# Encoder block on eight cores: the projection's rows transposed by DMA, early weight loads tied to matmuls, another order of the first rows

## What is computed

```python
u = rms_norm(h, g_mix)
z = u @ w_in                                   # value | gate | pool | gate A | gate B, 1024 columns each
gates = sigmoid(z[..., c3:] + b_gate)
a = depthwise_conv31(z_val * sigmoid(z_gate)) + b_dw
y_conv = silu(layer_norm(a)) @ w_conv_out
m = window_mean(z_pool, windows 2, 4, 8, 16 by channel group) - z_pool
y_pool = (per_group(m @ w_pool) * pool_scale) @ w_pool_out
h = h + (gates_A * y_conv + gates_B * y_pool) @ w_o      # output projection
v = rms_norm(h, g_ffn)
h = h + (silu(v @ w_ffn_gate) * (v @ w_ffn_up)) @ w_ffn_down     # hidden width 2816
out = rms_norm(h, g_final)
```

## Time and profile before

| | us |
|---|---|
| kernel, median of 3 runs | 1040.3 (1039.11 to 1068.77) |
| the profiled execution, its own time | 1040.15 |
| its span, slowest core (core 0) | 1038.6 |
| spans of the eight cores | 1034.1 to 1038.6 |
| busy: PE, DVE, ACT, POOL | 1010.3, 429.4, 296.3, 176.6 |

### The profile page before, as it was taken

The page is one execution under the profiler, slowest core; times in us unless marked ns, Lnnn a source line. Parts: engine busy times, 40 slices in busy tenths (PEclk is TensorE's granted clock), DMA queues, the critical chain, the costliest instruction groups (busy, mean ns, idle before and its releaser), DMA issues.

```text
span 1038.6 us, 16871 instructions; the slowest of 8 cores (1034.1 to 1038.6 us)
## 1 busy us (share of the span) xinstructions
PE 1010.3 (97%) x5900; PEld 498.3 (48%) x5900; DVE 429.4 (41%) x630; ACT 296.3 (29%) x521; POOL 176.6 (17%) x329
## 2 busy tenths in 40 slices
PE   6879999999999999999999999999999999999996
PEld 2545555444454444444456555544445444444442
DVE  4445545742472233221345565574247121211133
ACT  4324455512152222211113334551215211111111
POOL 2411122011122112210231111101112211111010
PEclk9999999999999999999999999999999999999999
DMA  9998795363339968640939879335332955554022
GB/s 227 154 246 176 145 208 81 77 97 55 68 124 170 153 114 132 95 74 1 172 98 249 190 145 172 53 79 93 61 64 79 153 73 80 80 74 71 1 72 101
DMA packets 68148, 118.37 MB, mean 114 GB/s; under 512 B 18465, under 2 KB 18465, under 8 KB 68066
## 3 DMA queue, kind: packets, MB, share of 16 engines
q0 software_dynamic: 38592, 70.27, 44.1%
q1 hardware_dynamic: 27170, 38.90, 13.8%
q10 hardware_dynamic: 2304, 8.13, 2.0%
HBM read 159.72 MB, written 8.39 MB: 162 GB/s over the span
## 4 chain that ended last, share of the span: by engine, by line
PE 93%; DMA 3%; SPq 2%; issue 1%; DVE 1%; ACT 0%; DVEq 0%; POOL 0%; POOLq 0%; ACTq 0%
PE ps L378 87%; PE ps L511 5%; SPq L214 2%; DMA wr<-wst 1%; DMA rep<-aT 1%; PE ps L410 1%; DMA h<-xe 1%; DVE ub L400 0%; DVEq L922 0%; ACT sqj L388 0%; POOL stats L391 0%; ACT uT L421 0%; ACT sqj L732 0%; DVE h L730 0%; DVE aT L481 0%
## 5 line engine op out<-in xcount | busy, mean ns | idle before, releaser
L378 PE MATMUL ps<-vT,wr 128*128 128x512 bf16 x1408 | 304.9, 379 | 0.0
L378 PE MATMUL ps<-uT,wr 128*128 128x352 bf16 (+2 forms) x1664 | 292.9, 335 | 4.8 <-DMA wr<-wst 4.2
L214 POOL DMA_DIRECT2D wr<-wst x268 | 143.4, 538 | 695.5 <-PE ps L378 638.3
L378 PEld LDWEIGHTS ps<-uT,wr 128*128 128x128 bf16 x1664 | 161.9, 98 | 132.2 <-issue 15.9
L378 PEld LDWEIGHTS ps<-vT,wr 128*128 128x128 bf16 x1408 | 137.5, 98 | 164.7
L378 PE MATMUL ps<-wr,fT 128*128 128x512 bf16 x704 | 152.3, 379 | 0.0
L712 DVE TENSOR_TENSOR fT<-ps,sgf 128x512 bf16<-128x512 f32 x88 | 60.8, 691 | 217.2 <-PE ps L378 191.8
L711 ACT ACTIVATE sgf<-ps 128x512 f32<-128x512 f32 x88 | 52.5, 597 | 227.9 <-PE ps L378 227.9
L378 PEld LDWEIGHTS ps<-wr,fT 128*128 128x128 bf16 x704 | 68.9, 98 | 83.1
L511 PE MATMUL ps<-rep,wr 128*32 128x512 bf16 x1024 | 59.9, 388 | 6.5 <-DMA rep<-aT 5.7
L732 ACT ACTIVATE sqj<-h 128x512 bf16<-128x512 f32 x32 | 20.1, 630 | 134.0 <-DVE h L730 134.0
(11 more groups left out here) (70 smaller groups left out, 639.2 us busy)
## 6 DMA issues: line engine op xcount, KB each, us to landing
wr<-wst POOLq DMA_DIRECT2D x268, 256.0 KB, 6.4
rep<-aT SPq DMA_DIRECT2D x256, 65.8 KB, 5.8
xt<-xe SPq DMA_DIRECT2D x24, 512.0 KB, 4.4
out<-h ACTq DMA_DIRECT2D x15, 512.0 KB, 2.6
h<-xe SPq DMA_DIRECT2D x8, 512.0 KB, 8.7
wpt<-wpt SPq DMA_DIRECT2D x4, 256.0 KB, 9.8
gb_s<-gb SPq DMA_DIRECT2D x2, 512.0 KB, 9.2
xt<-xe SPq DMA_DIRECT2D x2, 128.0 KB, 5.7
```

Source lines behind the costliest of these rows:

```text
L214: e.dma_start(out=o[1], in_=o[2]).then_inc(o[3], 16)
L378: S.op(PE, lambda e: e.matmul(out, lhsT=lhsT, rhs=rhs, start=start, stop=stop), [lhsT, rhs], [out], signal=signal)
```

## The change

Three things. (1) Rows out of the output projection are transposed by DMAs from SP (`v_transpose`), each one row behind the projection, in both tiles; the PE transposes and their evictions go. Every transpose gets its own semaphore, 17 in all. (2) While `lead` is below 21, `rel` first makes POOL wait until PE has finished all that was written out for it so far. (3) `START` has another order: G10, H10, G11 and H11 come after the transposes of rows 7 and 8, two weight loads come later and two fewer fall into the start, R0 comes before the last four matmul units; one idle group is gone, `idle_mm(4)` is `idle_mm(2)`, and row 0's mean square is taken between the two copies of `gb`.

```diff
--- before.py
+++ after.py
@@ -42,8 +42,8 @@
 P2_STEPS = ["G0", "G1", "P0", "P1", "G2", "P2", "G3", "Y0.0", "Y1.0", "Y2.0", "Y0.1", "Y1.1", "Y2.1", "P3", "Y3.0", "Y3.1"]
 for _c in range(4, KC):
     P2_STEPS += [f"G{_c}", f"P{_c}", f"Y{_c}.0", f"Y{_c}.1"]
-START = """L3 I4 A0 B0 T0 I4 L4 A1 E0d W1 B1 T1 I4 L5 A2 E1d W1 B2 T2 A3 E2d B3 G00 T3 L6 A4 E3a W1 B4 H00 T4 L7 A5 E4d W1 B5
-V00 G10 T5 C0 A6 E5a W1 B6 H10 G01 T6 A7 E6d W1 B7 V10 H01 T7 A8 E7a V01 B8 G11 H11 T8 W2 E8d G02 H02 V11 V02 R0
+START = """L3 B0 T0 I4 L4 A1 E0d B1 T1 I4 L5 A2 E1d B2 T2 A3 E2d B3 G00 T3 L6 A4 E3a W1 B4 H00 T4 L7 A5 E4d W1 B5
+V00 T5 C0 A6 E5a B6 G01 T6 A7 E6d W1 B7 H01 T7 A8 E7a V01 W1 B8 G10 T8 W2 H10 E8d G02 H02 V10 G11 H11 V02 R0 V11
 G12 H12 V12 S0""".split()
 
 
@@ -325,7 +325,7 @@
     POOL = Rec("pool", sem("s_pool"))
     SP = Rec("sp", sem("s_sp"))
     gb_sem = [Prod(sem(f"d_gb{i}"), 16) for i in range(3)]
-    tr_sem = [Prod(sem(f"d_tr{i}"), 16) for i in range(2)]
+    tr_sem = [Prod(sem(f"d_tr{i}"), 16) for i in range(17)]
     wpt_sem = [Prod(sem(f"d_wpt{i}"), 16) for i in range(2)]
     cst = [Prod(sem(f"d_cst{i}"), 16) for i in range(3)]
     ring_sem = [Prod(sem(f"d_wr{i}"), 16) for i in range(RING)]
@@ -363,6 +363,8 @@
 
     def rel(k=1):
         wstate["freed"] += k
+        if wstate["lead"] < RING:
+            S._waits(POOL, {PE: PE.count})
         room = wstate["li"] + wstate["lead"] - wstate["next"]
         if room > 0:
             prefetch(min(room, k + 1))
@@ -451,7 +453,7 @@
     def s0_transpose(i, idx):
         r, n = SUBS[idx]
         n = (n + 15) // 16 * 16
-        xbar_transpose(SP, tr_sem[idx % 2], uT[:, :, r:r + n], ub[idx % NUB][0:n, :])
+        xbar_transpose(SP, tr_sem[idx], uT[:, :, r:r + n], ub[idx % NUB][0:n, :])
 
     COLS = [(0, 352), (352, 352), (704, 351)]
 
@@ -694,6 +696,9 @@
                                                                               op0=ALU.mult, op1=ALU.add), [poi, xi], [ho])
         if s + 3 < 8:
             xres_load(i, s + 3)
+
+    def v_transpose(s):
+        xbar_transpose(SP, tr_sem[9 + s], vT[:, :, s * 128:(s + 1) * 128], ub[s % NUB][:])
 
     ff_w = {}
     fi = [0]
@@ -787,12 +792,6 @@
         for j in range(k):
             mm(psum[b_][:], zt[:, 0:128], zt[:], True, True, j == k - 1)
 
-    idle_mm(4)
-    for h in range(2):
-        b_ = nb()
-        g_i, g_p, g_o = grow[:, h * 512:(h + 1) * 512], psum[b_][:], gb[:, 0, h * 512:(h + 1) * 512]
-        mm(g_p, ones[0:1, :], g_i, True, True, True)
-        S.op(DVE, lambda e, g_o=g_o, g_p=g_p: e.tensor_copy(out=g_o, in_=g_p), [g_p], [g_o])
     rs0 = {}
 
     def row_a(k):
@@ -811,6 +810,19 @@
     def row_e(k, eng):
         r, n = SUBS[k]
         transpose_evict(n, uT, r, tb[k], eng)
+
+    idle_mm(2)
+    gbp = []
+    for h in range(2):
+        b_ = nb()
+        g_i, g_p = grow[:, h * 512:(h + 1) * 512], psum[b_][:]
+        mm(g_p, ones[0:1, :], g_i, True, True, True)
+        gbp.append(g_p)
+    for h in range(2):
+        g_p, g_o = gbp[h], gb[:, 0, h * 512:(h + 1) * 512]
+        S.op(DVE, lambda e, g_o=g_o, g_p=g_p: e.tensor_copy(out=g_o, in_=g_p), [g_p], [g_o])
+        if h == 0:
+            row_a(0)
 
     vb = {}
     for st in START:
@@ -886,14 +898,13 @@
             if s >= 1:
                 norm_scale(h1[s - 1][:], 128, 1, (s - 1) % NUB, prs)
             prs = rms_rstd(h1[s][:], 128)
-            if s >= 2:
-                norm_transpose(128, vT, (s - 2) * 128, (s - 2) % NUB)
+            if s >= 1:
+                v_transpose(s - 1)
         norm_scale(h1[7][:], 128, 1, 7 % NUB, prs)
+        v_transpose(7)
         rel(8)
         ffn(0, 0)
-        norm_transpose(128, vT, 6 * 128, 6 % NUB)
         ffn(1, 0)
-        norm_transpose(128, vT, 7 * 128, 7 % NUB)
         ffn(2, 0)
         ffn(0, 1)
         ffn(1, 1)
```

## The result

| | before | after |
|---|---|---|
| median, us | 1040.3 (1039.11 to 1040.34) | 1057.8 (1057.28 to 1059.27) |
| the profiled execution, its own time | 1040.15 | 1057.28 |
| its span, slowest core | 1038.6 (core 0) | 1055.6 (core 6) |
| spans of the eight cores | 1034.1 to 1038.6 | 1047.2 to 1055.6 |

The ratio of the times is 1.017, with a 95% interval of 1.015 to 1.019. The forecast was 1027.7 us, a gain of 12.6; the kernel lost 17.5. The sign was wrong, and 1057.8 lies far outside the range of 1023.5 to 1033.5. In some executions the cores of one die run slower throughout, at a lower clock; these are left out of the times, and on the one chip where it was always so, cores 0 to 3 of the other die are compared alone.

What follows compares the result with a forecast made beforehand. PE was taken to bound the kernel, busy 1010.3 of 1038.6 us. The sum was 1040.15 - 6.4 (DMA transposes) - 3.9 - 1.7 (held early loads) - 0.5 (start order) = 1027.65, forecast 1027.7 us, range 1023.5 to 1033.5.

Steps and rivals of the forecast that it cites:

- the landing of row 7's transpose: Ahead of the fourth ffn group: landing in 2.7 to 6.6 us, so 0.4 us of stall per tile, 0.8 us together.
- The cover: PE's work after the projection's last matmuls, three ffn groups of 3.45 us, 10.35 us, hides row 7's transpose.
- Rival C: Row 7's transpose served after rel(8)'s eight loads: landing 17.5 us, PE stall 11.8 us per tile, 1050.5 us; chance 0.10.
- Part 1's gain: Output projection: 16 rows each lose 0.45 us of PE transposes, 7.2 us saved before any stall.
- Part 2: At conv(1): copies land sooner, so no wait, -3.9 us, and no clock drop, -1.7 us.
- rival B: At conv(1): copies still take 9.2 us because of SP's queue, PE waits 2.5 us, clock falls, 1031.9 us; chance 0.15.
- The last issue of group 1: SP's last shifted copy for conv(1), issued at 64.8 us, comes 0.8 to 2.5 us earlier.
- Part 3: Reordered start brings conv(0) forward by 1.8 us or nothing; taken as -0.5 us.
- T8 at 35.0 us, not 36.28: In the start: moving G10 and H10 back brings row 8's transposes 1.3 us forward.
- Equal, if the clock does not fall: The start ends at 43.85 us against 43.8 before; 1.7 us later if the clock falls.
- the prediction's own sign that it is wrong: In the start: the lower clock covering more than 3.4 us would show the prediction wrong.
- Rival E: Some 12 weight loads now come after conv(3); conv(7) waits up to 1.5 us, clock drop 1.7, 1031 us; chance 0.10.

Runs made afterwards that it cites:

- the run with 14 loads: Changed kernel, tile 0 with six unread loads behind the eight of rel(8), tile 1 with four of eight held; tile 0 landing 16.9 to 19.4 us.
- the loads held: Changed kernel, POOL issuing rel(8)'s eight loads only after row 7's transpose landed: 1030.6 us, again 1030.9; with the old start order 1028.0.
- part 2 by itself: Kernel before with only the early weight loads made to wait for PE's progress: 1033.2 us, ratio 0.9932.
- the kernel with 1039.2: Changed kernel with PE transposes back in place of the DMA transposes: 1039.2 us, ratio 0.9992.
- Part 1 alone: Kernel before with only the projection's rows transposed by DMA, old start order, no wait on early loads: 1060.07 us in its one usable execution.

## Why the prediction was wrong, and where it was right

**The step that failed is the landing of row 7's transpose**, "I take 0.4 us for each of the two tiles, 0.8 us". It landed after 13.6 to 19.0 us; on the slowest core that made 22.6 us of stall and 4.6 of lower clock behind it. The cover (10.35 us, measured 10.5) and the landing time at which it would be used up (5.7 us, measured 19.0 - 13.5 = 5.5) were right, and so was the place. Wrong was the duration: 2.7 to 6.6 us came from nine transposes spread over 110 us, none with a burst of eight loads beside it. The DMA view of before from issue to landing of three of them (331.91 to 338.49, 388.28 to 393.96 and 442.35 to 445.08 us) shows what their times went with:

```profile
q0 software_dynamic: 417, 0.75, 66.8%
...
q0 software_dynamic: 298, 0.54, 65.6%
...
q0 software_dynamic: 115, 0.20, 40.5%
```

At 144 packets a load these are 2.9, 2.1 and 0.8 loads, with landings of 6.6, 5.7 and 2.7 us. So the 6.6 was not the worst with DMA full but the time beside three loads, and eight were to come. "DMA share 1.04" said that the engines were busy, not with how many packets of which size.

**Rival C** had the place, the mechanism's outline, nearly the size (17.5 us against 13.6 to 19.0, 1050.5 against 1057.8) and far too small a chance, 0.10. Its reason was slightly off: after a late first packet the transpose is served in turn with the loads, not behind them, which the run with 14 loads tells apart; with eight, both come to nearly the same landing. It left out the lower clock that follows a stall of this length, although show such a drop after a wait of 3.9 us; with 4.6 us for it C would have given 1055.1. It was to cost more than the gain from a landing of 12.4 us on, and the measured ones lie above that on every core.

The Trainium skill has the rule in DMA: Bandwidth & Descriptors, "Queues, rings and completion order": each DMA engine goes round the queues it has work for and switches between packets. The page's packet is a group of some 9 to 17 descriptors; whether the profile counts the same unit no run shows. The trace agrees with the turns, with 303 packets of either queue in 4 us, but not with turns from the issue on, as the first packet came 4.1 to 5.5 us after it. The rule that the prediction weighed instead, 1309 ns for each 128x128 block (VectorE: DVE Perf Modes, "The three transpose paths"), did not hold here: eight blocks landed in 3.0 to 3.6 us when no load stood beside them.

**Part 1's gain** was right: rows 3.47 us apart, SP and DVE hidden. With the loads held it brought 8.7 us in the new order and 1033.2 - 1028.0 = 5.2 in the old one (over the profiled cores' mean spans 8.4 and 6.6), around the predicted 7.2.

**Part 2** was right in mechanism and a bit small in size: 5.6 predicted, 7.3 measured. The copies were the loads' victims, so rival B fell for part 2 by itself: 6.0 us to land, 5.5 assumed. Together with the new order B came half true on the slowest core, 7.5 us to land and a wait of 2.1, though the clock didn't fall. The last issue of group 1, forecast 0.8 to 2.5 us earlier, came at 65.4 us against 64.8. The surplus fits conv(0), whose wait went too, which the sum had left out. A wait of 1.9 us stayed at conv(1), but without a clock drop.

**Part 3** was taken at -0.5 and measured at +0.8 to +1.8 alone, but +2.9 (held) and +6.0 us (1039.2 against 1033.2, without DMA transposes) once part 2 had freed the copies. Two steps failed. "T8 at 35.0 us, not 36.28": with G10 away, T5 comes 0.9 us sooner, but `ub` of row 8 sets T8, 36.59 us. And "Equal, if the clock does not fall" set the new order at full clock against the kernel before with its clock drop; at full clock in both it is 23.1 us against 20.1 from T8 to conv(0). Besides, the cores had 6.8 to 10.2 us of lower clock where the sum priced one drop of 3.4 at most; lower clock for more than 3.4 us of the start was the prediction's own sign that it is wrong. So after has 61.32 us at conv(0), not 58.1 to 59.9.

**Rival E** did not come: PE does not wait for copies at conv(6) or conv(7) in any profile.

**The account** of the profiled executions, 1040.15 to 1057.28: conv(7) ends 2.1 us earlier, the transposes save 7.2, the stalls cost 22.6, the clock behind them 4.6. That makes +17.9 where 17.1 were measured; the 0.8 between them are not assigned.

**What stays open.** Why row 7's first packet comes 4.1 to 5.5 us after its issue beside the loads. Why the clock falls more often in the new order; its drops vary from core to core. Why the new order costs 6.0 us in one pair and 2.9 in the other: the mean spans of the profiled cores differ by 4.5 and 3.4, and in the kernel with 1039.2 the two slowest cores wait 2.1 and 2.2 us at conv(1) with a clock drop behind it, but that is one execution. Part 1 alone has no timed ratio, only one execution.

## What to carry to other kernels

When a transfer of many small packets meets a stream of large ones from another queue, count packets, not bytes: each of its packets can wait for one of the others, and a median of quiet cases says nothing of a burst. Hold a burst of prefetches behind the small transfer that a stage waits for, if the prefetches have slack; here one wait was worth 27 us. Before work is moved behind a point of the program, see what sets the time of that point: here it did not come earlier, and the work moved behind it cost its full time. And price a stall of several microseconds with the lower clock that follows it.

## What the runs showed of the hardware

- A DMA transpose of 128x1024 in bf16 carries its data in 1024 packets of 256 B. It lands after 3.0 to 3.6 us with the loads held, 7.8 to 10.9 beside four loads (128 packets of 2048 B each), 13.4 to 19.0 beside eight, 16.9 to 19.4 beside fourteen. Its first packet is served 1.1 to 1.2 us after the issue with the loads held, 4.1 to 5.6 beside them.
- While both queues were served, they shared the engines packet for packet (303 against 303 in 4 us), so the one with the smaller packets got the smaller share of bytes: 0.08 MB against 0.55.
- In PE's gap of 13.5 us the clock fell to 0.50 while PE did nothing, and it was at a mean of 0.54 still from 328 to 332 us, with PE fully busy since 326.13.
